# Routing and expert 0's first loads in another order; in block 2 scores ahead of a split, and Silu and the retention weights later

## The reference, cut to what matters

```python
def moe_ffn(x, router_w, w1, w3, w2):
    logits = (xt @ router_w).astype(F32)
    top_v, top_i = lax.top_k(logits, TOP_K)
    top_w = jax.nn.softmax(top_v, axis=-1)
    gates = jnp.sum(jax.nn.one_hot(top_i, N_EXPERTS, dtype=F32) * top_w[..., None], axis=1)
    for e in range(N_EXPERTS):
        y = y + gates[:, e:e + 1] * swiglu(xt, w1[e], w3[e], w2[e])
x = layer_norm(ALPHA * x + h, ln1_g[l], ln1_b[l])
x = layer_norm(ALPHA * x + f, ln2_g[l], ln2_b[l])
```

```python
o = _layernorm(o, ones).reshape(B, S, H * DV) * gn_gain
return jax.nn.silu(g) * o
```

## Time and profile before

| | |
|---|---|
| median of three runs | 2469.07 us (2467.51 to 2471.76) |
| profiled execution, own time | 2477.02 us |
| its span | 2475.2 us |
| busy, PE / DVE / ACT / POOL | 98% / 79% / 59% / 1% of the span |
| chain that ended last | PE 93%, DVE 4%, ACT 1%, issue 1% |
| moved by DMA | 626.17 MB, mean 253 GB/s |

### The profile page before, as it was taken

How to read it: one execution, slowest core, us unless ns; L and a number is a source line. 1 busy time by engine, 2 the same in 40 slices (tenths; PEclk the granted TensorE clock), 3 DMA queues, 4 the chain that set the end, 5 groups by cost and what they waited for, 6 DMA issues and landing times.

```text
span 2475.2 us, 29836 instructions
## 1 busy us (share of the span) xinstructions
PE 2435.4 (98%) x11602; PEld 2013.1 (81%) x11602; DVE 1963.0 (79%) x2458; ACT 1453.1 (59%) x1504; POOL 31.7 (1%) x44
## 2 busy tenths in 40 slices
PE   9999999999999999999999999899999999999998
PEld 7788877788888888888888888688888888888887
DVE  4855567999989988898889898799875568997645
ACT  4344443677777777777777777356445445654543
POOL 0000000000000000000000000000000000000000
PEclk9999998999999999999999999999999999999999
DMA  8366553899999999999999998554556656445663
GB/s 268 102 222 187 162 171 108 306 348 363 371 358 343 363 371 358 342 364 371 358 342 364 370 356 322 168 170 120 171 178 192 190 175 204 120 154 177 197 190 124
DMA packets 274155, 626.17 MB, mean 253 GB/s; under 512 B 17899, under 2 KB 27255, under 8 KB 273880
## 3 DMA queue, kind: packets, MB, share of 16 engines
q1 hardware_dynamic: 271708, 615.92, 72.8%
q0 software_dynamic: 1872, 6.82, 0.8%
q10 hardware_dynamic: 428, 1.45, 0.2%
HBM read 623.06 MB, written 1.07 MB: 252 GB/s over the span
## 4 chain that ended last, share of the span: by engine, by line
PE 93%; DVE 4%; ACT 1%; issue 1%; DMA 0%; POOLq 0%; POOL 0%; ACTq 0%; DVEq 0%
PE tile L765 28%; PE tile L767 28%; PE tile L766 28%; PE aux L887 4%; DVE units_parts L1982 1%; PE aux L1173 1%; PE aux L1388 1%; PE aux L1300 1%; DVE zbuf L2617 0%; PE aux L1088 0%; PE aux L1193 0%; PE aux L1194 0%; PE tile L920 0%; PE aux L1445 0%; PE aux L1313 0%
## 5 line engine op out<-in xcount | busy, mean ns | idle before, releaser
L1982 DVE TENSOR_TENSOR units_parts<-units,high 128x1024 fp32r<-128x1024 f32 (+3 forms) x369 | 551.7, 1511 | 87.5 <-ACT high L1516 82.2
L1516 ACT ACTIVATE high<-units 128x1024 fp32r<-128x1024 f32 (+3 forms) x369 | 470.3, 1290 | 172.0 <-PE tile L767 71.6
L766 PE MATMUL tile<-units_parts,acts 128*128 128x512 f32 (+2 forms) x1456 | 559.9, 385 | 0.0
L765 PE MATMUL tile<-high,acts 128*128 128x512 f32 (+2 forms) x1068 | 423.6, 397 | 5.9 <-DVE units_parts L1982 3.2
L767 PE MATMUL tile<-high,acts 128*128 128x512 f32 (+2 forms) x1068 | 412.1, 386 | 0.0
L766 PEld LDWEIGHTS tile<-units_parts,acts 128*128 128x128 f32 x1456 | 276.1, 190 | 50.9 <-issue 1.0
L766 PE MATMUL tile<-units_parts,zbuf_parts 128*128 128x512 f32 x616 | 239.8, 389 | 0.0
L765 PEld LDWEIGHTS tile<-high,acts 128*128 128x128 f32 x1068 | 201.7, 189 | 45.7 <-DVE units_parts L1982 5.3
L767 PEld LDWEIGHTS tile<-high,acts 128*128 128x128 f32 x1068 | 201.5, 189 | 41.1
L767 PE MATMUL tile<-high,zbuf_parts 128*128 128x512 f32 x508 | 197.9, 390 | 0.0
L765 PE MATMUL tile<-high,zbuf_parts 128*128 128x512 f32 x436 | 171.1, 393 | 0.0
(11 more groups left out here) (436 smaller groups left out, 4987.4 us busy)
## 6 DMA issues: line engine op xcount, KB each, us to landing
units<-in_moe_w SPq DMA_DIRECT2D x216, 1024.0 KB, 5.3
units<-in_w_in SPq DMA_DIRECT2D x134, 512.0 KB, 3.8
units<-in_w_ff SPq DMA_DIRECT2D x128, 512.0 KB, 3.6
q_buf<-in_moe_w SPq DMA_DIRECT2D x54, 1024.0 KB, 5.5
k_buf<-in_moe_w SPq DMA_DIRECT2D x54, 1024.0 KB, 5.4
nat<-in_moe_w SPq DMA_DIRECT2D x54, 1024.0 KB, 5.3
units<-in_ffn_w SPq DMA_DIRECT2D x48, 512.0 KB, 3.7
units<-in_w_out SPq DMA_DIRECT2D x32, 512.0 KB, 3.5
```

The lines of the kernel that those rows point to most:

```text
L765: nc.tensor.matmul(bank, lhs[0], high, start=start, stop=False)
L766: nc.tensor.matmul(bank, lhs[0], low, start=False, stop=False)
L1516: nc.scalar.activation(high_slot(SG[0], n) if wide_ else high_slot(SG[0], n)[:, 0:cols], halves(weights) if wide_ else weights[:, 0:cols], ...
L1982: V.tensor_tensor(low, weights, high, ALU.subtract).then_inc(SG[0].low_ready, 1)
```

## The change

It has two parts. In block 1, layer 1: SP issues the first two units of expert 0 (to q_buf and k_buf) as soon as the last attention scores are taken (`SCORED1`), ahead of the last w_out unit; the router's parts are made in this layer, just ahead of the layer norm, twice over in 256 columns, and each router matmul takes 128 of these columns, of which 16 count; q_buf is split ahead of the layer norm too, and ACT takes its high part ahead of the block's; `layer_norm` puts block 1's normalisation between the low parts of block 0's halves; PE turns block 1's first half, multiplies block 0's, and so on; `keep_busy` is 4 + 1 ahead and 2 behind (before: 2 and 4); each block's logits are taken by one reduction, and block 0's on their own; the rank's matrices are in one part (5 matmuls for 10); expert 0 waits for its gathered banks two by two; `acc` is computed at tile 1 of round 0, and `find_extra` runs at tile 3 of round 2. In block 2: the third scores are taken ahead of the split, three taps move from step 5 to step 13, the retention gate is evacuated as a copy and gets its Silu behind the last exponential, Sigmoid comes at head 0, and the weights are multiplied in at head 2.

```diff
-ROTATE_AT, ROTATED_AT, NSA_AT, GAIN_AT = (2, 3), 6, 10, 13
+ROTATE_AT, ROTATED_AT, NSA_AT, GAIN_AT = (2, 3), 6, 10, 2
-TAPS_STEP = [2, 2, 0, 0, 2, 4, 6, 4] + [4] * 8
+TAPS_STEP = [2, 2, 0, 0, 2, 1, 6, 4] + 5 * [4] + [7, 4, 4]
+EXPERT_FIRST, SCORED1 = 2, 104
...
@@ SP
-                wide(S, A["w_out"][l], 0, D)
...
+                    wide(S, A["w_out"][l], 0, D - P)
+                    sp.wait_ge(S.aux_full, SCORED1)
+                    units(0, 0, EXPERT_FIRST, len(STREAM1))
+                    wide(S, A["w_out"][l], D - P, P)
+                    C.unit.take(EXPERT_FIRST)
...
@@ PE
-                    for b in range(TB):
-                        if b == 0:
-                            keep_busy(2, sums_at[-1])
-                        else:
-                            turned_at[True, 4, b] = C.aux.n
-                            turn_block(x, b, 4)
...
-                                mm = nc.tensor.matmul(bank[:, 0:2 * N_EXP], part,
-                                                      router_parts[:, c, :, :].rearrange("p i e -> p (i e)"),
+                                mm = nc.tensor.matmul(bank[:, 0:P], part, router_row[:, c * 16:c * 16 + P],
...
-                    keep_busy(4)
+                    keep_busy(4, sums_at[-1])
+                    pe.wait_ge(router_ready, 1)
+                    turned_at[True, 4, 1] = C.aux.n
+                    keep_busy(1, sums_at[-1])
+                    turn_half(x, 1, 0, 4)
+                    second, bank = aux_bank(), aux_bank()
+                    route(bank, 0, 0)
+                    turn_half(x, 1, 1, 4, second)
+                    route(bank, 0, 1).then_inc(S.aux_full, 1)
+                    bank = aux_bank()
+                    route(bank, 1, 0)
+                    route(bank, 1, 1).then_inc(S.aux_full, 1)
+                    keep_busy(2)
+                    pe.wait_ge(rank_parts, 2)
                     pe.wait_ge(route_mask, 1)
...
                     def expert(r, _):
-                        aux_done()
+                        if r > 0:
+                            aux_done()
                         for t in range(MOE_TILES):
-                            tile_e(tiles[2 * t % 4], gathered[place_of(r)])
+                            tile_e(tiles[2 * t % 4], gathered[place_of(r)],
+                                   C.aux.n - 4 if (r, t) == (0, 0) else None)
...
@@ ACT
+                    ahead(END[0] - 2)
+                    for part, whole in ((before_r, before), (ones_r, ones[:, :])):
+                        nc.scalar.activation(part, whole, ACT.Copy).then_inc(rank_parts, 1)
                     highs_block(True, 4, 0)
-                    ahead(END[0] - 2)
+                    ahead(END[0] - 1)
                     highs_block(True, 4, 1)
-                    ahead(END[0] - 1)
...
-                    func = ACT.Sigmoid if t >= 7 and t != 8 else ACT.Silu if t == 5 else ACT.Copy
+                    func = ACT.Sigmoid if t >= 7 and t != 8 else ACT.Copy
...
                     if u == UNITS2 - 1:
                         act.wait_ge(S2.tile_evac, C.tile.n)
-                        nc.scalar.activation(sig[0], sig[0], ACT.Sigmoid)
+                        nc.scalar.activation(z[:, 5, :, :], z[:, 5, :, :], ACT.Silu).then_inc(swish_ready, 1)
...
                         high_of(br_t[0][0][:, :, P:2 * P], turned_at["nsa", l, 1])
+                        nc.scalar.activation(sig[0], sig[0], ACT.Sigmoid)
...
@@ DVE
-                    block_in(0)
+                    half_in(0, 0)
+                    normal_block(1, x, second)
+                    half_in(0, 1)
+                    block_in(1)
                     between()
...
+                    for at in (slice(0, KC), slice(KC, 2 * KC)):
+                        step(V.tensor_copy(router_parts[:, at, 0, :], router[:, :, :]))
+                        ins = V.tensor_tensor(router_parts[:, at, 1, :], router[:, :, :], router_parts[:, at, 0, :],
+                                              ALU.subtract)
+                    ins.then_inc(router_ready, 1)
+                    split(len(STREAM1) + 1)
+                    layer_norm(2, ALPHA, lambda: logits_at.extend([C.aux.take(), C.aux.take()]))
...
-            split(len(STREAM1) + 1)
             for b, n in enumerate(logits_at):
                 dve.wait_ge(S.aux_full, n + 1)
...
-                step(V.tensor_copy(logits[:, b, :], bank[:, N_EXP:2 * N_EXP]))
-                V.tensor_tensor(logits[:, b, :], logits[:, b, :], bank[:, 0:N_EXP],
-                                ALU.add).then_inc(S.aux_evac[n % 4], 1)
+                V.tensor_reduce(logits[:, b, :], aux[n % 4][:, 0:2 * N_EXP].rearrange("p (i e) -> p e i", i=2),
+                                AX.X, ALU.add).then_inc(S.aux_evac[n % 4], 1)
...
+                    if (r, t) == (0, 1):
+                        V.tensor_scalar(acc[:, :, :], x[:, :, :], ALPHA, None, ALU.mult)
+                    if (r, t) == (2, 3):
+                        find_extra()
...
             lows_gathered([0])
-            V.tensor_scalar(acc[:, :, :], x[:, :, :], ALPHA, None, ALU.mult)
             split(len(STREAM1) + EXPERT_LEAD)
-            find_extra()
...
+                scores(2)
                 fill()
                 read_back()
                 for u in range(UNITS2):
-                    if u + 2 < UNITS2:
+                    if 0 < u < UNITS2 - 2:
                         scores(u + 2)
...
-                    if u == GAIN_AT:
-                        dve.wait_ge(tables_loaded, 16 * TABLES2 * (l + 1))
-                        evicted(5)
-                        for b in range(TB):
-                            V.tensor_tensor(z[:, 5, b, :], z[:, 5, b, :], ret_gn[:, :], ALU.mult)
...
+                    if h == GAIN_AT:
+                        dve.wait_ge(tables_loaded, 16 * TABLES2 * (l + 1))
+                        dve.wait_ge(swish_ready, l + 1)
+                        for b in range(TB):
+                            V.tensor_tensor(z[:, 5, b, :], z[:, 5, b, :], ret_gn[:, :], ALU.mult)
```

More of the change, by code:

```diff
@@ L367, in build @@
             rank = sb("rank", [P, TB, ROUNDS + 1], where=one)
-            mask = sb("mask", [P, TB, N_EXP], where=one)
+            mask = sb("mask", [P, TB, N_EXP], F32R, where=one)
             excess = sb("excess", [P, 2, N_EXP], where=one)
@@ L598, in hidden @@
                     wide(sig_, w2, part[0][0], sum(width for _, width in part))
-            def expert(r, named):
[L602 to L614, removed]
-                            unit(S, lambda v: v.rearrange("p (c n) -> p c n", c=EXPERT_CHUNKS),
-                                 w[r0:r0 + EXPERT_CHUNKS * P, t * 512:(t + 1) * 512].rearrange(
-                                     "(c p) n -> p c n", p=P))
-                        else:
-                            r0 = (m - 2 * MOE_TILES * TILE_UNITS) * EXPERT_ROWS * P
-                            unit(S, lambda v: v.rearrange("p (c n) -> p c n", c=EXPERT_ROWS),
-                                 w2[r0:r0 + EXPERT_ROWS * P, :].rearrange("(c p) n -> p c n", p=P))
@@ new lines, in matrices, with units @@
+            def matrices(e):
+                if isinstance(e, int):
+                    return [A[n][0, e] for n in ("moe_w1", "moe_w3", "moe_w2")]
+                return [A[n][0, bass.ds(e, 1)].rearrange("o k n -> (o k) n")
+                        for n in ("moe_w1", "moe_w3", "moe_w2")]
+            def units(e, first, last, n=None):
+                w1, w3, w2 = matrices(e)
+                for m in range(first, last):
+                    if m < 2 * MOE_TILES * TILE_UNITS:
+                        t, k = divmod(m, 2 * TILE_UNITS)
+                        w = w1 if k < TILE_UNITS else w3
+                        r0 = (k % TILE_UNITS) * EXPERT_CHUNKS * P
+                        unit(S, lambda v: v.rearrange("p (c n) -> p c n", c=EXPERT_CHUNKS),
+                             w[r0:r0 + EXPERT_CHUNKS * P, t * 512:(t + 1) * 512].rearrange(
+                                 "(c p) n -> p c n", p=P), None if n is None else n + m)
+                    else:
+                        r0 = (m - 2 * MOE_TILES * TILE_UNITS) * EXPERT_ROWS * P
+                        unit(S, lambda v: v.rearrange("p (c n) -> p c n", c=EXPERT_ROWS),
+                             w2[r0:r0 + EXPERT_ROWS * P, :].rearrange("(c p) n -> p c n", p=P))
@@ L1136, in _ @@
                 else:
-                    for b in range(TB):
-                        if b == 0:
-                            keep_busy(2, sums_at[-1])
-                        else:
-                            turned_at[True, 4, b] = C.aux.n
-                            turn_block(x, b, 4)
-                        bank = aux_bank()
-                        for c in range(KC):
-                            if c % 4 == 0:
-                                evacuated(turned_at[True, 4, b] + c // 4)
+                    assert scored_at[1, UNITS1 - 1] + 1 == SCORED1
@@ L2437, in _ @@
             for b in range(TB):
[L2438 removed]
```

(1 more changed line is left out.)

73 lines of the change are left out of this document (39 added, 34 removed).

## The result

The changed kernel's median is 2457.49 us (four runs, 2456.88 to 2458.03) against 2470.41 us for the kernel before (four runs, 2467.51 to 2475.24); the ratio is 0.9939, 95% interval 0.9925 to 0.9953. The profiled execution has a span of 2455.5 us.

The account below looks back on a forecast made before the run. The prediction took TensorE (PE), busy for 98% of the span, as the bound. Routing and first expert (4.3 us) plus block 2 (5.4) gave 9.7 us, from 2469.07 to 2459.4 us, range 2456.0 to 2466.5.

Parts of the forecast that it names:

- the likeliest case: Whole kernel: the forecast itself, a gain of 9.7 us to 2459.4 us, chance 0.58.
- Routing up to the gather: Block 1's router: full clock and an earlier, shorter chain let the gather start 2.5 us earlier.
- First expert: Start of expert 0: PE's 1.2 us wait on the last bank's low parts goes.
- Fourth unit and moved work: Expert 0's unit 3 split: with ALPHA copy and find_extra moved, PE's 0.6 us wait goes; moved work costs nothing.
- The other end: Experts, round 2: the moved copy and find_extra cost their whole 3.7 us there, instead of nothing.
- Block 2: Block 2, both layers: PE's waits on ACT's probabilities and DVE's scores go, 5.4 us in all.
- the value near the row's own waits: Block 2: 5.4 us chosen between nothing and 5.5, since each chain gives way by more than the wait.
- Rival 1: Router: the clock falls as before and is back by the gather; gain 7.2 us, 2461.9 us, chance 0.12.
- Rival 2: Router onwards: the clock stays down and the gather doubles; 2465.7 to 2472.5 us, chance 0.08, 0.02 for slower.
- Rivals 3 and 4: 3: DVE bounds block 2, half its gain lost, 2462.1, chance 0.15. 4: experts' earlier start lost, 2463.7, chance 0.07.
- The chances: Whole kernel against about 0.2% (4.9 us): faster 0.83, same 0.14, slower 0.03.

Follow-up runs that it names:

- e2: The kernel before with only the edits of block 2; 2463.62 us, ratio 0.9972.
- e6: The changed kernel with expert 0 waiting for all four gathered banks again; 2462.71 us in one run.
- e9: The kernel before with only the third scores of each layer of block 2 taken ahead of the split; 2470.69 us in one run.
- e10: The kernel before with only the gate's Silu behind the last exponential, Sigmoid at head 0 and the weights at head 2; 2471.01 us in one run.
- e1: The kernel before, unchanged, run again; 2473.19 us over 12 runs, ratio 1.0002.
- e4: The changed kernel with router matmuls of 16 columns in place of 128; 2461.05 us, ratio 0.9956.
- e11: The kernel before with only the router's 128 columns, parts made ahead of the layer norm, in the old order; 2474.09 us in one run.

## Why the prediction was wrong, point by point

The direction, the places and the likeliest case held; none of the rivals came true in the changed kernel. What failed was the sum's size, 9.7 us for a measured 11.8 in the stretches, above all in its term for block 2, and with it the range. Even with 11.8 the sum would give 2457.3, inside the range; the rest of the 15 us in the first four runs of each kernel is in no stretch that the profiles tell apart, and over all runs (13.3 us) the result would be 2455.8, just under the lower end.

- **Routing up to the gather: 2.5 forecast, 2.9 to 3.7 measured.** What was moved ahead of the layer norm cost nothing, as forecast: from the first w_out matmul to the first keep_busy PE needs 24.2 us before and 24.3 after. Every step of the chain is there, each 0.3 to 0.4 us ahead of the forecast (with the second sum of the last block, 428.42 before and 419.65 after, as the common start): the last 24 matmuls begin at 434.6 in the old time instead of 434.9 and cost 0.12 each as forecast, the mask ends at 439.05 instead of 439.4, the gather starts at 442.1 instead of 442.5. And the kernel before isn't always the one of the profile that was read: where its low clock lasted longer (e2), its router took 17.11.
- **First expert: 1.2 forecast, 1.4 measured (e6).** The gather's 3.84 us were added in full; the first expert matmul begins 3.60 behind its start, as it enters before the last one has ended.
- **Fourth unit and moved work: 0.6 forecast, 0.8 measured.** The other end (3.7 us lost in round 2) did not come: no PE wait in all experts.
- **Block 2: 5.4 forecast, 6.7 measured.** This is the term of the sum that was mis-sized most: "the value near the row's own waits". The waits are 5.5 us as listed, and with each of the six 0.1 to 0.2 us more go (e9 and e10; the taps by difference), mostly since the list counts a wait from the modelled end of the matmul before it. The prediction said that each chain gives way by more than the wait, and yet took slightly less than the waits. DVE took nothing back, for which 0.05 per layer had been taken off; the 1.85 us ahead of the last head became 0.64, Silu's and the weights' new places cost PE nothing.
- **The range.** It allowed 2 to 3 us for what single runs differ, read from three runs. 70 runs of the kernel before spread from 2464.8 to 2479.1 with a median of 2471.9; the three shown lay low among them. The profiled execution stood 8 us above them and 5.1 above the median of 70. It reaches layer 1's first score 4.7 us later than e1's, with low clock in the first 20 us (0.83) that e1 hasn't; the long low clock in attention is in five of the six profiles of the old first half without filling. The forecast carried this along and did not look into it, though a window row of it, 13.6 us at 0.50, stood in the earlier trace rows for another purpose.
- **The rivals.** Rival 1, the clock: not in any of nine profiles with the width and the new order, but in e4 as soon as the width goes. Rival 2: e11 shows its mechanism, with a router and first expert 2.0 us longer. Rivals 3 and 4: no wait in block 2 or in the experts.
- **The chances.** They don't add up: the forecast and rivals 1 and 3 are 0.85 together, and with over half of rival 4 some 0.89, where 0.83 stands for faster.

## What to carry to other kernels

A wait of PE in a nearly full pipeline costs what the list of waits gives and, here, 0.1 to 0.2 us more; over six short waits that was a sixth of the gain (1.2 of 6.7 us). Price a removed wait from start to start. Small matmuls held the clock here at no cost when they were made wide with columns that nobody reads (0.12 us each at 16 and at 128 columns), but where the work behind them didn't follow soon (e11), the clock fell one step later and took the next, larger piece with it. Before a difference of half a per cent is explained by one profile, compare unchanged stretches of several: here one of them moved by 7 us by itself.

## What was not expected of the hardware

Layer 1's attention takes 32.9, 34.4 or 40.0 us in the same instructions, with none, one or two stretches at the lower level; in that stretch small matmuls (64 to 256 columns) alternate with waits of 1.5 to 2.0 us. And a clock that falls one place later can be dearer than one that falls early: at the router it cost 2.8 us (e4), behind it the mask's matmuls and the gather (e11) lost more than the width had gained.
